# Third layer: loads, compression inputs and output splits moved, feed-forward products in eight banks

## The reference

```python
# layers 1 and 2
proj = rms_norm(x, g) @ w_in
ya = chunked gated delta rule over 4 heads, chunks of 64, with a short convolution
yb = windowed means over 2, 4, 8 and 16 positions, mixed per group
yc = attention of 4 heads over the 256 keys with the highest index score
x = x + (sum over n of sigmoid(gate_n) * (y_n @ w_branch_n)) @ w_out
# layer 3
proj = rmsnorm(h, norm1_w) @ w_in_2
kc, vc = gelu((32-position windows, stride 16, + pos) @ phi_w1) @ phi_w2   # 31 rows
o_nsa = g0 * attention(q, kc, vc) + g1 * attention(q, selected blocks) + g2 * window attention
o_lru = scan(a, b)(conv(xr)) * gelu(yr)      # 1024 channels, 8 blocks of 128
h = h + (gate1 * (o_nsa @ w_nsa_up) + gate2 * (o_lru @ w_lru_up)) @ w_o
h = h + square(relu(rmsnorm(h, norm2_w) @ w_ff1)) @ w_ff2
```

## Time and profile before

| | us |
|---|---|
| median of three runs | 2058.72 (2054.36 to 2059.23) |
| the profiled execution | 2057.2 |
| its span | 2055.4 |
| TensorE busy (matmuls) | 1995.9, 97% of the span |
| weight loads of TensorE | 1568.4, 76% |
| VectorE busy | 1071.6, 52% |
| ScalarE busy | 915.2, 45% |
| POOL busy | 871.8, 42% |
| DMA, mean | 111 GB/s |

### The profile page before, as it was taken

The page is one execution under the profiler, slowest core; times in us unless marked ns, Lnnn a source line. Parts: engine busy times, 40 slices in busy tenths (PEclk is TensorE's granted clock), DMA queues, the critical chain, the costliest instruction groups (busy, mean ns, idle before and its releaser), DMA issues.

```text
span 2055.4 us, 24487 instructions
## 1 busy us (share of the span) xinstructions
PE 1995.9 (97%) x9420; PEld 1568.4 (76%) x9420; DVE 1071.6 (52%) x1877; ACT 915.2 (45%) x1414; POOL 871.8 (42%) x646
## 2 busy tenths in 40 slices
PE   8999899999999999999999999999999999999999
PEld 6767778777788768787877787676777787888887
DVE  6756945645746657754464656677444256201210
ACT  5455443334335455443334355577455344412421
POOL 5444432334354445332434455456222345444443
PEclk9999999999999999999999999999999999999999
DMA  5234342323534244431424545322111232322332
GB/s 189 95 113 124 122 138 98 132 85 99 186 111 151 86 123 133 139 118 62 155 72 133 184 152 154 121 70 83 62 43 51 103 102 83 97 98 93 102 110 74
DMA packets 90916, 228.53 MB, mean 111 GB/s; under 512 B 25928, under 2 KB 29000, under 8 KB 89488
## 3 DMA queue, kind: packets, MB, share of 16 engines
q1 hardware_dynamic: 89360, 223.82, 33.6%
q10 hardware_dynamic: 1440, 3.15, 0.4%
HBM read 195.06 MB, written 24.64 MB: 107 GB/s over the span
## 4 chain that ended last, share of the span: by engine, by line
PE 72%; DVE 15%; ACT 6%; DMA 3%; issue 2%; SPq 1%; POOL 1%; ACTq 0%; DVEq 0%
PE bank L442 71%; DVE tmp L386 4%; PE bank L445 2%; DVE kv L376 1%; DVE E L376 1%; ACT tmp L428 1%; SPq L371 1%; ACT wh L431 1%; DVE lt L386 1%; DMA pad<-tmp 1%; DMA gt<-gates 1%; ACT pad L431 1%; DVE tmp L376 1%; DVE nacc L386 1%; ACT L420 0%
## 5 line engine op out<-in xcount | busy, mean ns | idle before, releaser
L376 POOL TENSOR_TENSOR wl<-st,wh 128x512 fp32r<-128x512 f32 x606 | 823.7, 1381 | 1101.2 <-ACT wh L431 1101.1
L442 PE MATMUL bank<-hh,wh 128*128 128x512 f32 x1632 | 666.9, 409 | 27.3 <-ACT tmp L428 10.7
L442 PE MATMUL bank<-hl,wh 128*128 128x512 f32 x1632 | 640.2, 392 | 0.0
L442 PE MATMUL bank<-hh,wl 128*128 128x512 f32 x1632 | 640.1, 392 | 0.0
L431 ACT ACTIVATE wh<-st 128x1024 fp32r<-128x1024 f32 x303 | 318.2, 1050 | 238.8 <-PE bank L442 196.6
L442 PEld LDWEIGHTS bank<-hh,wh 128*128 128x128 f32 x1632 | 308.7, 189 | 131.1 <-issue 43.8
L442 PEld LDWEIGHTS bank<-hl,wh 128*128 128x128 f32 x1632 | 309.1, 189 | 67.4 <-issue 7.2
L442 PEld LDWEIGHTS bank<-hh,wl 128*128 128x128 f32 x1632 | 308.7, 189 | 66.7
L376 DVE TENSOR_TENSOR xt<-xt,bank 128x512 f32<-128x512 f32 x40 | 27.4, 686 | 235.6 <-PE bank L442 235.6
L386 DVE SCALAR_TENSOR_TENSOR tmp<-pad,col,tmp 128x512 f32<-128x512 f32 x80 | 81.8, 1022 | 38.8 <-ACT tmp L428 36.8
L442 PE MATMUL bank<-fh,wh 128*128 128x512 f32 x256 | 99.6, 389 | 0.0
(11 more groups left out here) (340 smaller groups left out, 3008.6 us busy)
## 6 DMA issues: line engine op xcount, KB each, us to landing
st<-units SPq DMA_DIRECT2D x303, 512.0 KB, 3.5
gates<-tmp SPq DMA_DIRECT2D x48, 256.0 KB, 2.5
gt<-gates SPq DMA_DIRECT2D x48, 256.0 KB, 3.8
pad<-tmp SPq DMA_DIRECT2D x32, 128.0 KB, 4.5
qk<-tmp SPq DMA_DIRECT2D x16, 256.0 KB, 4.3
x_scratch<-xt SPq DMA_DIRECT2D x2, 2048.0 KB, 8.7
xt<-x_scratch SPq DMA_DIRECT2D x2, 2048.0 KB, 8.6
ph<-phi SPq DMA_DIRECT2D x8, 512.0 KB, 4.6
```

Of the source, the lines that this page charges most:

```text
L376: return NOTHING if self.e is None else self.e.tensor_tensor(out, a, b, op)
L442: return NOTHING if self.e is None else self.e.matmul(out, lhsT, rhs, start=start, stop=stop, skip_group_check=share)
```

## The change

- `CUTS` has seven positions instead of six, and the last value of `SELECT` is 3 instead of 5 (layers 1 and 2).
- SP: the loads of `ph`, `lw`, `p2` and `cau` move from ahead of `proj2` to its end, between the three takes of `v2`, so behind the exchanged rows.
- VectorE: the windows `zt` are written by `windows(j)` in the `v2` steps of `proj2` instead of in `compress`.
- `compress`: TensorE's transpositions and ScalarE's copy `hid` come one step later (ScalarE's by one as well), what follows stays at its step.
- `lru` on ScalarE: the first merge gate, `gate_of(0)`, comes one step earlier.
- The splits into `yh2` and `yl2` move from the head of `merge3` to the end of `nsa`.
- `ffn`: the `f1` products use banks j % 8. VectorE writes the low half of block j - 1 behind the square of block j.

```diff
@@ -24,9 +24,9 @@
...
-CUTS = (5, 9, 13, 16, 20, 24)
-SELECT = (8, 12, 5)
+CUTS = (4, 8, 11, 14, 17, 21, 25)
+SELECT = (8, 12, 3)
@@ -1091,13 +1091,13 @@
...
                 yield
-            yield from idle(6)
+            yield from idle(7)
             o = bank(5, "hid")
...
             t.then_inc(*sig("c_tr"))
-            yield from idle(4)
+            yield from idle(3)
             pe.wait_ge(*at("free5", "hid"))
@@ -1254,7 +1254,7 @@
...
                 for j in range(0 if half else 4, 16):
-                    for _ in tile(("f1", 16 * half + j), j % 4, ("f1", half, j), "nB"):
+                    for _ in tile(("f1", 16 * half + j), j % 8, ("f1", half, j), "nB"):
                         pass
@@ -1706,13 +1706,10 @@
...
             ac.act(ge[1][:], ge[1][:], ACT.Tanh, 0.7978845608028654 * 0.044715).then_inc(*sig("cg_a", 1))
-            yield
-            yield
-            yield
-            yield
+            yield from idle(5)
             ac.wait_ge(*at("c_tr"))
             ac.cp(hid[:].rearrange("p a b -> p (a b)"), banks[5][:, 0:256]).then_inc(*sig("free5", "hid"))
-            yield from idle(4)
+            yield from idle(3)
             x = ctile[0][:, 0:31]
@@ -1778,7 +1775,7 @@
...
             for n in range(3):
-                if n == 2:
+                if n == 1:
                     gate_of(0)
@@ -1854,12 +1851,13 @@
...
                 yield
-        def merge3():
             for c in range(4):
...
                 ac.cp(yh2[:, c, :], onT[:, c, :]).then_inc(*sig("yh2", c))
+            yield
+        def merge3():
             for m in range(8):
@@ -1875,7 +1873,7 @@
...
                         ac.wait_ge(*(at("fl", half, j - 4) if j >= 4 else at("fl", 0, 12 + j)))
-                        ac.act(r[:], banks[j % 4][:], ACT.Relu).then_inc(*sig(f"free{j % 4}", "f1", half, j))
+                        ac.act(r[:], banks[j % 8][:], ACT.Relu).then_inc(*sig(f"free{j % 8}", "f1", half, j))
                     ac.wait_ge(*at("f_sq", half, j))
@@ -2388,28 +2386,26 @@
...
             for j in range(3):
-                if j == 2:
+                if j < 2:
+                    windows(j)
+                else:
                     for b in range(4):
...
+        def windows(j):
+            a, b = names[("posk", "posv")[j]]
+            pos = col[:, a:b]
+            dv.wait_ge(*at(f"kg{j}", 3))
+            for g in range(2):
+                for f in range(2):
+                    view = kg[:, j, g, 16 * f:16 * f + 496].rearrange("p (n m) -> p m n", m=16)[:, 0:16:2, :]
+                    t = dv.tt(zt[:, 8 * f:8 * f + 8, j, 31 * g:31 * g + 31], view, pos[:, 8 * f:8 * f + 8].unsqueeze(2).broadcast_to([128, 8, 31]), ALU.add)
+            t.then_inc(*sig("cz", j))
         def compress():
-            def rows(j):
-                a, b = names[("posk", "posv")[j]]
-                pos = col[:, a:b]
-                dv.wait_ge(*at(f"kg{j}", 3))
-                for g in range(2):
-                    for f in range(2):
-                        view = kg[:, j, g, 16 * f:16 * f + 496].rearrange("p (n m) -> p m n", m=16)[:, 0:16:2, :]
-                        t = dv.tt(zt[:, 8 * f:8 * f + 8, j, 31 * g:31 * g + 31], view, pos[:, 8 * f:8 * f + 8].unsqueeze(2).broadcast_to([128, 8, 31]), ALU.add)
-                t.then_inc(*sig("cz", j))
-            yield
-            rows(0)
-            yield
-            rows(1)
-            yield from idle(2 + 8)
+            yield from idle(2 + 2 + 8)
             dv.wait_ge(*at("cg_a", 0))
@@ -2567,6 +2564,10 @@
...
+        def squares_low(half, j):
+            dv.wait_ge(*at("fh", half, j))
+            dv.tt(fl[:, j, :], tmp[j % 4][:], fh[:, j, :].bitcast(F32), ALU.subtract).then_inc(*sig("fl", half, j))
         def ffn():
@@ -2575,10 +2576,11 @@
...
                         dv.stt(r[:], banks[j][:], 0.0, nr[:], ALU.max, ALU.mult).then_inc(*sig(f"free{j}", "f1", 0, j))
-                    dv.wait_ge(*at(f"free{j % 4}", "f1", half, j))
+                    dv.wait_ge(*at(f"free{j % 8}", "f1", half, j))
                     dv.tt(r[:], r[:], r[:], ALU.mult).then_inc(*sig("f_sq", half, j))
-                    dv.wait_ge(*at("fh", half, j))
-                    dv.tt(fl[:, j, :], r[:], fh[:, j, :].bitcast(F32), ALU.subtract).then_inc(*sig("fl", half, j))
+                    if j > 0:
+                        squares_low(half, j - 1)
+                squares_low(half, 15)
                 for m in range(8):
@@ -2853,7 +2855,15 @@
...
             yield from lagged(jobs())
-            take(3)
+            for i in range(3):
+                inner(i)
+            take()
+            for c in range(2):
+                sp.dma(lw[c][:], lruw[:, :, c, :]).then_inc(*dma(f"lw{c}", c))
+            take()
+            sp.dma(p2[:], phi2).then_inc(*dma("b2_in", "p2"))
+            sp.dma(cau[:], cd_d).then_inc(*dma("b2_in", "cau"))
+            take()
@@ -2931,12 +2941,6 @@
...
         sp.wait_ge(*at("kz0"))
-        for c in range(2):
-            sp.dma(lw[c][:], lruw[:, :, c, :]).then_inc(*dma(f"lw{c}", c))
-        for i in range(3):
-            inner(i)
-        sp.dma(p2[:], phi2).then_inc(*dma("b2_in", "p2"))
-        sp.dma(cau[:], cd_d).then_inc(*dma("b2_in", "cau"))
         for _ in proj2():
```

## The result

The changed kernel takes 2039.77 us (median of 4 runs, 2035.53 to 2041.28), the kernel before on the same chip 2056.54 (4 runs): the ratio is 0.9915, 95% interval 0.9893 to 0.9937, 16.8 us less between the medians. The forecast was 2043.5 with a range of 2031 to 2053. Run again on another chip it gave 2038.25 (5 runs) against 2057.67 (21 runs), ratio 0.9910 [0.9896, 0.9923]. The profiled execution took 2041.28, its span is 2039.5 (before 2055.4), and TensorE is busy 98% of it.

What follows compares the result with a forecast made beforehand. TensorE, busy 97% of the span, was taken as the bound, with gains only in its gaps: 8.0 + 3.7 + 3.5 = 15.2 us off 2057.2 gives 2042.0, against the median 2043.5; range 2031 to 2053.

Steps and rivals of the forecast that it cites:

- Loads and windows: Third layer: later loads remove the 1.38 us gap, 1.5 us; earlier windows remove the 2.89 gap and clock spell, 4.6.
- Rival B: The recurrence is the chain from its first block; 4.6 and 1.5 come back as waits, 7.2 us stay, 2051.5; chance 0.17.
- Transpositions and gate: Third layer: gaps of 4.24 and 2.45 us go, but the recurrence's chain leaves gains of only 1.6 and 0.3 us.
- Rival A: Every gap is independent, so the gains in all three layers add: 29.8 us, 2028.9; chance 0.15.
- Output splits: After the third layer's last kept tile: the 2.02 us gap and its 1.7 us clock loss go, 3.7 us.
- Feed-forward: Feed-forward part, eight banks and later low half of the square: no gap to remove, 0 us, bounds -1 and +1.
- Cuts: Layers one and two: VectorE's inverse starts one step earlier, winning 1.8 and 1.7 us, together 3.5.
- SELECT: Last selection, layers one and two: the 1.19 us gap goes but TensorE then stands some 2.5 us elsewhere; 0 us.
- Rival D: Slower by the clock: if eight new TensorE waits each cost 3.4 us, 12 us slower, 2070; chance 0.04.

## Why the prediction was right, step by step

**Loads and windows.** Predicted 1.5 + 4.6, measured 1.9 + 4.6, alone 6.2 by the ratio. The q copies were done by 1247.7 where 1251 was the mark (3.1 us of that were won earlier, so the mark was met by little), no gap took the place of the 2.89, and no wait appeared in the v2 steps. The 4.6 hold the spell of the kernel before, as the prediction's sum does: of the seven profiles with the old windows four have it, and against one without it the windows bring some 3 us. The rule of the Trainium skill (DMA: Bandwidth & Descriptors, Two DMAs through the same engine are not ordered), taken to mean that the unit behind the ph loads comes late, had no effect on the time: the units loaded from 1262 to 1276 landed 3.5 to 4.5 us after their issue, before 3.4 to 3.6, and TensorE waited for none. Rival B falls with this part.

**Transpositions and gate.** Predicted -1.9, measured +1.0, alone a ratio of 1.0001. The mechanism was right: the recurrence on ScalarE and VectorE is the chain there, and the new waits stand where they were named, 2.61, 1.96 and 2.87 us. The term was too large: I gave TensorE the 1.6 us that ScalarE had stood for it, and left the spells out that follow the new waits; 0.5 of the 1.6 came, and 1.5 were lost at lup where I had a gain of 0.3. POOL's low half of the last block, the bound that I had named, is the measure of the chain:

```profile
1420.00 1.54 POOL L376 TENSOR_TENSOR ol<-nacc,oh 128x512 fp32r<-128x512 f32 x1
```

That is a row of the changed kernel, 10.2 us sooner than before, of which 3.1 were there at mark 183: the chain itself gained 7.1 us, what the loads and windows alone bring (7.1). At lup TensorE then loses 1.5. Rival A falls here: 11.7 us of gaps went and brought nothing.

**Output splits.** Predicted -3.7, measured -3.9 in a profile where before had the spell. Of the eight profiles with the old splits four had it; where it is missing the stretch is 1.6 us shorter and the splits bring 2.3. They were not run alone, so this part rests on the stretch and on the gap that is gone from it.

**Feed-forward.** Predicted 0 with the words "No gap to remove"; measured -3.2. This is the step of the prediction that failed, a term put at nothing. The window that I read begins at 1732, 8 us behind a gap of 2.99 us, whose releaser the timeline gives only as issue. The gap lay in the stretch that the edit touches: product five takes bank 0, which VectorE reads at 1723.12 behind the last normalised tiles. The window said that the products run at full rate once they run, not that the first ones start in time.

**Cuts.** Predicted 1.8 + 1.7, measured 4.3 and -0.8 in one profile, 3.3 and 2.2 in the other, 6.4 alone. The 4.2 us gaps were to shrink to about 3; they are gone. The start of the inverse was placed well (198.2 predicted, 198.49 measured):

```profile
192.39 2.37 DVE L392 MEMSET lT<- 32x512 f32 x4 [1.50 <-DMA blocks<-lT]
...
198.49 0.19 DVE L376 TENSOR_TENSOR E<-kv 128x31 f32<-128x31 f32 x1 [3.73 <-DMA kv<-blocks]
```

From it I took off the work that falls into the inverse's span, 1.9 us of selection. In the first layer the start comes 4.9 us sooner, the span holds 5.7 us more of other work, and the inverse's own instructions are 6.1 us shorter: the end comes 5.3 us sooner. That part of the term, the duration of the pieces, was held constant, and it isn't. By the Trainium skill's rule (SBUF — State Buffer, SBUF: two separate sides) a VectorE instruction with two SBUF inputs and a GpSimd one that reads SBUF exclude each other. The traces agree in that each slow instruction lies beside one of POOL's, and less well in that a few of the others do too; no run kept POOL away from the inverse, so this cause is read from the rows and not isolated. That this would cost the change its gain was the wrong sign: in all seven profiles with the changed kernel's cuts 5 or 6 instructions are slow in a layer, in all six with the old cuts 10 to 13. What I had not named is the readback. With the cuts alone it ends last in both layers (2.46 and 3.10 us); the changed kernel waits 3.05 us for it in the second layer, with 3.4 us of clock behind, in the first profile, and 0.86 and 0.98 in the second. Why it differs between two profiles of one kernel stays open.

**SELECT.** Predicted 0. The gaps are 1.0 us shorter in sum where neither has a spell, and 0.6 longer where the new one has it. Ten of the twelve passes with the new placing have a spell there, five of the sixteen with the old: 1.0 less 1.6 x (0.83 - 0.31) is 0.2 us a layer, nothing.

**The sum.** 15.2 was forecast and 15.9 read between the spans. That they lie so near is luck, because misses cancel: 2.9 too much for transpositions and gate, 3.2 too little for the feed-forward part. Alone, cuts, loads with windows, and feed-forward give 6.4 + 6.2 + 4.7, with 3.9 for the splits 21 us; together 16.8 to 19.4, which the intervals of the single runs allow. Rival D counted the waits well (five of its eight came, four of them with a spell) and priced them badly: each of these spells costs 1.7 us, not 3.4, and three of the waits fall where the recurrence ends last anyway.

## What to carry to other kernels

Before an edit is costed at nothing, list the idle rows of the whole stretch that it touches, its first instructions among them, and ask of each which resource it waits for; a window of steady work hides the wait in front of it. Two gaps of 4.24 and 2.45 us on the busiest engine were worth nothing, since a chain on two other engines ran beside them, and 2.99 us needed two edits of which each alone is worth nothing. When work is moved on an engine whose instructions grow beside another's, don't carry its durations over.

## What the hardware showed that I had not expected

After the same gap the clock sometimes falls and sometimes doesn't, and the longer the gap, the more often it falls. Over all fourteen profiles (timeline of TensorE behind 100 us, with the granted clock beside it) a spell at 1.2 GHz began by 2 us behind the gap's end in:

| gap, us | gaps | with a spell | of them 6.83 us long |
|---|---|---|---|
| 0.75 to 1.25 | 130 | 4 | 0 |
| 1.25 to 1.75 | 21 | 1 | 0 |
| 1.75 to 2.25 | 28 | 15 | 0 |
| 2.25 to 3.25 | 53 | 42 | 3 |
| 3.25 and more | 24 | 24 | 14 |

The others are 3.41 us long, and each costs half its length. The gaps are those of a few places in fourteen nearly equal kernels, so the table tells of these places and not of any gap. One gap of 2.72 us, in the changed kernel's first layer, cost 1.7 us in one execution and none in the other. This is a part of the spread of 7.7 us that 26 runs of the kernel before showed on one chip (2054.27 to 2061.95): the three with a mean granted clock of 0.994 or more took at most 2056.42, the three at 0.990 or less at least 2058.48. How large a part isn't shown. The prediction's "a gap of 2.0 us or more is followed by a spell" was read from too few rows.
